# Dealing out the K and Q chains of an attention preparation step by step

## The chip, the cores and the metric

The program runs on the 8 cores of one Trainium2 chip. Each core computes one sample of a batch of 8 with the same program, and no core talks to another. The metric is the device time of the slowest core in microseconds, from one launch to the end. A core has five engines that run side by side, each with its own queue of instructions that it takes in order: TensorE (PE in the profile; PEld is its weight load), VectorE (DVE), ScalarE (ACT), GpSimd (POOL) and SyncE (SP, which here only issues DMAs). They meet through semaphores.

## The reference, cut to what matters

The reference is two layers of a hybrid backbone over 2048 latent tokens and 256 context tokens. The second layer has a multi-head latent attention with 8 heads. Before the attention, queries, keys and values are made from compressed vectors. This preparation is where the change lies:

```python
def mla_q(cq, q_norm, w_uq, qn_gain, angles):
    q = ((rms(cq) * q_norm) @ w_uq).reshape(b, l, N_HEADS, QK_HEAD)      # 768 -> 8 x 96
    q = rms(q) * qn_gain
    return axial_rope(q, *angles)

def mla_kv(ckv, k_rope, kv_norm, w_uk, w_uv, kn_gain, angles):
    ckv_n = rms(ckv) * kv_norm                                           # 256
    k_nope = (ckv_n @ w_uk).reshape(b, l, N_HEADS, QK_NOPE)              # 8 x 64
    v = (ckv_n @ w_uv).reshape(b, l, N_HEADS, V_HEAD)                    # 8 x 64
    k_r = broadcast(k_rope over the heads)                               # 8 x 32
    k = rms(concatenate([k_nope, k_r])) * kn_gain
    return axial_rope(k, *angles) if angles is not None else k, v
```

Keys and values are made for latent and context tokens, queries for latent tokens only, and only the 32 last elements of a head are rotated.

## The kernel before, in words

The program is recorded in stages: modulation vectors, a first mixer, a mixture of experts, then the second layer's mixer with an input projection, an S5 scan, the MLA preparation and attention, and a second mixture of experts. Between stages every engine waits for all others.

Python functions record the instructions. The calls `P.mm`, `P.tr`, `P.act`, `P.dve`, `P.pool` and `P.dma` append an instruction to one engine's list, in the order of the calls, and add a semaphore wait wherever a name in `reads` or `writes` was last touched by another instruction. Nothing reorders the lists later: the order of the Python calls is the order on each engine. `P.mm` writes lines L117 and L119 of the profile, `P.tr` line L125, `P.dma` line L135.

The MLA preparation is the first half of `_cd_mla`. It loops over 18 tiles of 128 tokens: 16 latent tiles with a K and a Q chain, then 2 context tiles with a K chain only. Each tile's compressed vectors (`ckt`, `cqt`) are loaded a tile ahead by GpSimd's queue (`c1_loads`). A chain is:

1. projection on TensorE into PSUM (`psm`): four matmuls for K and V, twelve for Q (six of 512 columns, six of 256);
2. evacuation by ScalarE with the row's scale (L1298 V, L1302 K, L1322 and L1324 Q); VectorE copies the shared rope part into K (L1305);
3. `norm_rope`: squares on GpSimd (L1245), reduction per head on VectorE (L1246), a small scaling (L1247), a square root on ScalarE (L1249), a reciprocal (L1250), two multiplies over 768 elements (L1251, L1253), the rotation (L1256, four small ones L1260, L1264), and a cast of the unrotated part by ScalarE (L1266; L1269 for context tiles);
4. `transpose_store`: eight transposes on TensorE into PSUM (`pst`), a copy by VectorE (L1275) and a store to DRAM by SyncE.

The loop records the whole K chain of a tile, transposes and store included, and then its whole Q chain. `sq`, `hs`, `R1` and `R2` are single buffers that both chains use; `xb` and `xst` are two buffers that take turns; PSUM banks come from rotations `nps` (six) and `npt` (two). `run_zip` stands in the program already: it steps up to `width` generators in turn, one `yield` each.

Of the kernel before, what the change touches and what calls it, by code (L numbers as in the profile page):

```python
# [1184 lines left out]
def _cd_mla(P, G, nc, mst):  # L1185
    AX = mybir.AxisListType.X
    QSCALE = 96.0 ** -0.5
    with ExitStack() as c1:
# [17 lines left out]
        hs = C(_sb(nc, "hs", [128, 4, 8], F32))
        R1 = C(_sb(nc, "R1", [128, 8, 32], F32))
        R2 = C(_sb(nc, "R2", [128, 8, 32], F32))
        xb = [C(_sb(nc, "xb%d" % s, [128, 8, 96], BF16)) for s in range(2)]
        xst = [C(_sb(nc, "xst%d" % s, [128, 8, 128], BF16)) for s in range(2)]  # L1210
# [33 lines left out]
        def norm_rope(src, sk, gain, gk, dst, dk, t, rope):
            P.pool(lambda e: e.tensor_tensor(out=sq[:], in0=src[:], in1=src[:], op=ALU.mult), reads=[sk], writes=["sq"])  # L1245
            P.dve(lambda e: e.tensor_reduce(out=hs[:, 0, :], in_=sq[:], axis=AX, op=ALU.add), reads=["sq"], writes=["hs"])  # L1246
            P.dve(lambda e: e.tensor_scalar(out=hs[:, 1, :], in0=hs[:, 0, :], scalar1=1.0 / 96, scalar2=EPS, op0=ALU.mult,  # L1247
                                            op1=ALU.add), reads=["hs"], writes=["hs"])
            P.act(lambda e: e.activation(out=hs[:, 2, :], in_=hs[:, 1, :], func=AF.Sqrt), reads=["hs"], writes=["hs"])  # L1249
            P.dve(lambda e: e.reciprocal(out=hs[:, 3, :], in_=hs[:, 2, :]), reads=["hs"], writes=["hs"])  # L1250
            P.dve(lambda e: e.tensor_tensor(out=src[:], in0=src[:], in1=hs[:, 3, :].unsqueeze(2).to_broadcast([128, 8, 96]),  # L1251
                                            op=ALU.mult), reads=[sk, "hs"], writes=[sk])
            P.dve(lambda e: e.tensor_tensor(out=src[:], in0=src[:], in1=gain[:, :].unsqueeze(1).to_broadcast([128, 8, 96]),  # L1253
                                            op=ALU.mult), reads=[sk, gk], writes=[sk])
            if rope:
                P.dve(lambda e: e.tensor_tensor(out=R1[:], in0=src[:, :, 64:96],  # L1256
                                                in1=ropC[:, t, :].unsqueeze(1).to_broadcast([128, 8, 32]), op=ALU.mult),
                      reads=[sk, "rop"], writes=["R1"])
                for (o0, i0) in ((0, 72), (8, 64), (16, 88), (24, 80)):
                    P.dve(lambda e, o0=o0, i0=i0: e.tensor_tensor(  # L1260
                        out=R2[:, :, o0:o0 + 8], in0=src[:, :, i0:i0 + 8],
                        in1=ropS[:, t, o0:o0 + 8].unsqueeze(1).to_broadcast([128, 8, 8]), op=ALU.mult),
                        reads=[sk, "rop"], writes=["R2"])
# [24 lines left out]
        c1_loads(0)
        for t in range(NT):
            s = t % 2  # L1290
            rkv = mst[:, t, 4:5]
# [2 lines left out]
            pkk, psk = nps()
            P.mm(psk[:, :], [(ckt[s][:, k, :], wk[:, k, :]) for k in range(2)], reads=[("ckt", s), "wqkv"], writes=[pkk])
            pkv, psv = nps()
            P.mm(psv[:, :], [(ckt[s][:, k, :], wv[:, k, :]) for k in range(2)], reads=[("ckt", s), "wqkv"], writes=[pkv])
            P.act(lambda e, s=s, psv=psv, rkv=rkv: e.activation(  # L1298
                out=vst[s][:, :, 0:64], in_=psv[:, :].rearrange("p (h e) -> p h e", h=8), func=AF.Identity, scale=rkv),
                reads=[pkv], writes=[("vst", s)])  # L1300
            P.dma("sp", G.vs[t], vst[s][:], reads=[("vst", s)], writes=["dram_v"], semkey="vst%d" % s)
            P.act(lambda e, s=s, psk=psk, rkv=rkv: e.activation(  # L1302
                out=kf[s][:, :, 0:64], in_=psk[:, :].rearrange("p (h e) -> p h e", h=8), func=AF.Identity, scale=rkv),
                reads=[pkk], writes=[("kf", s)])
            P.dve(lambda e, s=s, t=t: e.tensor_copy(out=kf[s][:, :, 64:96],  # L1305
                                                    in_=mst[:, t, 8:40].unsqueeze(1).to_broadcast([128, 8, 32])),
                  writes=[("kf", s)])
            u = ui % 2
            ui += 1
            norm_rope(kf[s], ("kf", s), GK, "GK", xb[u], ("xb", u), t, t < NT_L)  # L1310
            transpose_store(xb[u], ("xb", u), xst[u], ("xst", u),
                            G.ks[:, :, t * 128:(t + 1) * 128].rearrange("h d n -> d h n"), "xst%d" % u)
            if t < NT_L:
                rq = mst[:, t, 3:4]
                qfl = qf[s][:].rearrange("p h e -> p (h e)")
                pka, psa = nps()
                P.mm(psa[:, :], [(cqt[s][:, k, :], wq[:, k, 0:512]) for k in range(6)], reads=[("cqt", s), "wqkv"],
                     writes=[pka])
                pkb, psb = nps()
                P.mm(psb[:, 0:256], [(cqt[s][:, k, :], wq[:, k, 512:768]) for k in range(6)],  # L1320
                     reads=[("cqt", s), "wqkv"], writes=[pkb])
                P.act(lambda e, qfl=qfl, psa=psa, rq=rq: e.activation(out=qfl[:, 0:512], in_=psa[:, :], func=AF.Identity,  # L1322
                                                                      scale=rq), reads=[pka], writes=[("qf", s)])
                P.act(lambda e, qfl=qfl, psb=psb, rq=rq: e.activation(out=qfl[:, 512:768], in_=psb[:, 0:256],  # L1324
                                                                      func=AF.Identity, scale=rq),
                      reads=[pkb], writes=[("qf", s)])
                u = ui % 2
                ui += 1
                norm_rope(qf[s], ("qf", s), GQ, "GQ", xb[u], ("xb", u), t, True)
                transpose_store(xb[u], ("xb", u), xst[u], ("xst", u),  # L1330
                                G.qs[:, :, t * 128:(t + 1) * 128].rearrange("h d n -> d h n"), "xst%d" % u)
# [78 lines left out]
```

How the kernel before makes its waits and increments, by code:

```python
    def _wait(self, X, ev):  # L61
        if ev is None:
            return
        kind, k, v = ev
        key = (kind, k)
        if X.waited.get(key, 0) >= v:
            return
        X.waited[key] = v
        sem = self.eng[k].sem if kind == "e" else self.dsem[k][0]
        X.ins.append(lambda e, sem=sem, v=v: e.wait_ge(sem, v))
        X.sim.append(("w", key, v))
# [20 lines left out]
    def op(self, en, fn, reads=(), writes=()):  # L92
        X = self.eng[en]
        self._deps(X, reads, writes)
        X.tick += 1
        sem = X.sem
        X.ins.append(lambda e, fn=fn, sem=sem: fn(e).then_inc(sem, 1))
        X.sim.append(("i", ("e", en), 1))
        self._commit(("e", en, X.tick), reads, writes, en)
# [10 lines left out]
    def mm(self, out, pairs, reads=(), writes=()):  # L110
        X = self.eng["pe"]
        self._deps(X, reads, writes)
        n = len(pairs)
        sem = X.sem
        for i, (l, r) in enumerate(pairs):
            if i == n - 1:
                X.ins.append(lambda e, l=l, r=r, i=i: e.matmul(out, l, r, start=(i == 0), stop=True).then_inc(sem, 1))
            else:
                X.ins.append(lambda e, l=l, r=r, i=i: e.matmul(out, l, r, start=(i == 0), stop=False))
        X.tick += 1
        X.sim.append(("i", ("e", "pe"), 1))
        self._commit(("e", "pe", X.tick), reads, writes, "pe")
```

## Time and profile before

| what | us |
|---|---|
| median of 6 runs (range) | 11719.06 (11355.41 to 12172.02) |
| the profiled execution, its own time | 11356.62 |
| its span on the slowest core | 11355.1 |
| the other cores' spans | 11321.0 to 11354.5 |
| the MLA preparation's 16 latent tiles, first K matmul to the first one behind them | 527.66 |
| TensorE busy over the span | 8082.0 |

The page gives, for the slowest core, how long each engine is busy, the span in 40 slices, and the costliest groups of instructions with the time that the engine stood idle before them and what ended it. A timeline row has the start in us, the duration in us, engine, line of the program, operation, destination and sources (buffer numbers left out), shapes, and in brackets the idle time before it and who ended it.

### The profile page before, as it was taken

To read this page: it belongs to the slowest core of one execution; us is meant where nothing else is said; L and a number is where in the kernel's file an instruction comes from. 1 tells how busy PE (TensorE), PEld (TensorE's weight loads), DVE (VectorE), ACT (ScalarE), POOL (GpSimd) and SP (SyncE) were. 2 spreads that over 40 slices of the span, in tenths; PEclk is the share of its full clock that TensorE was granted. 3 is DMA by queue.
4 is the path that set the end of the run, shared out by engine and by line. 5 is a ranking of instruction groups with operands and counts; after the bars stand their busy time and mean duration, and the time that the engine had idled before them with its cause. 6 is when DMAs were issued, how large, how long until landed. Compare 5 with 4: busy or idle time off the path is not lost. (4 is left out here: it accounts for less than half of the span.)

```text
span 11355.1 us, 123247 instructions; the slowest of 8 cores (11321.0 to 11355.1 us)
## 1 busy us (share of the span) xinstructions
PE 8082.0 (71%) x37576; PEld 3873.0 (34%) x37576; DVE 6038.8 (53%) x9756; ACT 2191.6 (19%) x3933; POOL 839.7 (7%) x785
## 2 busy tenths in 40 slices
PE   7766489999999999761111111236667999999998
PEld 5322344444444444530000000113333444444443
DVE  0443356666666666117777777330034666666666
ACT  1312311111111111122222222116521111111110
POOL 0000000000000000002222222110000000000000
PEclk8887599999999999575555555557668999999999
DMA  3210022222222211210000000111102222222221
GB/s 108 30 25 15 1 45 34 34 34 34 32 32 34 33 30 20 74 39 1 3 1 3 1 3 3 42 24 28 39 16 41 38 35 43 36 40 39 34 41 45
DMA packets 335979, 344.18 MB, mean 30 GB/s; under 512 B 117427, under 2 KB 262067, under 8 KB 335352
## 3 DMA queue, kind: packets, MB, share of 16 engines
q0 software_dynamic: 200240, 226.18, 13.1%
q1 hardware_dynamic: 135112, 110.12, 3.3%
q8 instruction: 335, 5.49, 0.2%
q14 instruction: 292, 2.39, 0.1%
HBM read 529.35 MB, written 28.74 MB: 49 GB/s over the span
## 5 line engine op out<-in xcount | busy, mean ns | idle before, releaser
L119 PE MATMUL psu_u<-tT_u,wu_u 128*128 128x512 bf16 (+1 forms) x8064 | 1835.1, 367 | 56.7 <-DVE he_u L651 50.3
L119 PE MATMUL psg_u<-tT_u,wg_u 128*128 128x512 bf16 (+1 forms) x8064 | 1837.7, 368 | 49.0 <-DMA wg_u<-moe_w_gate 49.0
L119 PE MATMUL psy_u<-wd_u,he_u 128*128 128x512 bf16 x6528 | 1763.1, 379 | 56.2 <-DVE tmpe_u L356 56.2
L651 DVE TENSOR_TENSOR he_u<-sg_u,psu_u 128x512 bf16<-128x512 f32 (+1 forms) x1152 | 753.7, 657 | 1853.4 <-PE psu_u L117 1849.7
L356 DVE SCALAR_TENSOR_TENSOR tmpe_u<-psy_u,gates_u,gtile_u 128x512 f32<-128x512 f32 x2176 | 1624.1, 746 | 58.5 <-PE psy_u L117 58.5
L649 ACT ACTIVATE sg_u<-psg_u 128x512 f32<-128x512 f32 (+1 forms) x1152 | 660.8, 574 | 5103.7 <-PE psg_u L117 2502.5
L359 DVE TENSOR_TENSOR xl_u<-xl_u,tmpe_u 128x512 f32<-128x512 f32 x2176 | 1506.4, 692 | 226.3
L119 PEld LDWEIGHTS psg_u<-tT_u,wg_u 128*128 128x128 bf16 x8064 | 789.7, 98 | 915.3 <-issue 55.4
L119 PEld LDWEIGHTS psu_u<-tT_u,wu_u 128*128 128x128 bf16 x8064 | 786.9, 98 | 922.5 <-issue 68.4
L119 PEld LDWEIGHTS psy_u<-wd_u,he_u 128*128 128x128 bf16 x6528 | 619.9, 98 | 881.1 <-issue 180.2
L117 PE MATMUL psy_u<-wd_u,he_u 128*128 128x512 bf16 x2176 | 824.5, 379 | 0.0
L119 PE MATMUL pss_u<-s5hr_u,lc_u 128*128 128x512 bf16 x128 | 74.9, 585 | 833.9 <-DVE s5hi_u L1145 804.5
L125 PE MATMUL pss_u<-ident_u,bb_u 128*128 128x128 f32 x64 | 29.3, 458 | 828.0 <-DVE bb_u L1034 828.0
L125 PE MATMUL psm_u<-ident_u,xn_u 128*128 128x128 f32 x560 | 225.4, 441 | 403.7 <-DVE xn_u L298 341.1
L117 PE MATMUL psg_u<-tT_u,wg_u 128*128 128x512 bf16 (+1 forms) x1152 | 423.5, 368 | 0.0
L117 PE MATMUL psu_u<-tT_u,wu_u 128*128 128x512 bf16 (+1 forms) x1152 | 423.5, 368 | 0.0
L125 PE MATMUL pst_u<-identb_u,xb_u 128*96 128x128 bf16 x272 | 84.6, 311 | 381.6 <-ACT xb_u L1266 328.2
L135 POOL DMA_DIRECT2D wg_u<-moe_w_gate x64 | 56.6, 885 | 3813.1 <-PE psg_u L117 3562.8
L119 PEld LDWEIGHTS pss_u<-s5hr_u,lc_u 128*128 128x128 bf16 x128 | 13.3, 104 | 921.3 <-issue 921.3
L1374 ACT ACTIVATE pT_u<-psS_u 128x512 bf16<-128x512 f32 x576 | 318.5, 602 | 43.4 <-PE psO_u L816 29.0
L117 PEld LDWEIGHTS psy_u<-wd_u,he_u 128*128 128x128 bf16 x2176 | 212.4, 98 | 257.2
L125 PEld LDWEIGHTS pss_u<-ident_u,bb_u 128*128 128x128 f32 x64 | 11.6, 182 | 836.3 <-issue 834.3
(300 smaller groups left out, 8357.1 us busy)
## 6 DMA issues: line engine op xcount, KB each, us to landing
wg_u<-moe_w_gate POOLq DMA_DIRECT2D x64, 1024.0 KB, 10.5
wu_u<-moe_w_up POOLq DMA_DIRECT2D x64, 1024.0 KB, 14.6
wd_u<-moe_w_down POOLq DMA_DIRECT2D x64, 1024.0 KB, 8.2
adaw_u<-ada_w SPq DMA_DIRECT2D x24, 2048.0 KB, 7.9
xl_u<-x SPq DMA_DIRECT2D x1, 8192.0 KB, 30.6
out<-xl_u SPq DMA_DIRECT2D x1, 8192.0 KB, 24.3
wB_u<-ab_w_in POOLq DMA_DIRECT2D x24, 256.0 KB, 6.0
zs_scr<-zst_u SPq DMA_DIRECT2D x48, 128.0 KB, 1.7
```

The costliest lines, as they stand in the source:

```text
L117: X.ins.append(lambda e, l=l, r=r, i=i: e.matmul(out, l, r, start=(i == 0), stop=True).then_inc(sem, 1))
L119: X.ins.append(lambda e, l=l, r=r, i=i: e.matmul(out, l, r, start=(i == 0), stop=False))
L125: self.op("pe", lambda e: e.transpose(out, in_, ident), reads, writes)
L135: X.ins.append(lambda e: e.dma_start(out=out, in_=in_, **kw).then_inc(sem, 16))
L356: P.dve(lambda e: e.scalar_tensor_tensor(out=tmp[:, 0:n], in0=ps, scalar=gate, in1=gt[:, r, c0:c0 + n], op0=ALU.mult, op1=ALU.mult), reads ...
L359: P.dve(lambda e: e.tensor_tensor(out=G.xl[:, t, c0:c0 + n], in0=G.xl[:, t, c0:c0 + n], in1=tmp[:, 0:n], op=ALU.add), reads=[tk, ("xl", t) ...
L649: P.act(lambda e, cs=cs, n=n: e.activation(out=sg[cs][:, 0:n], in_=psg[cs][:, 0:n], func=AF.Silu), reads=[("psg", cs)], writes=[("sg", cs)])
L651: P.dve(lambda e, cs=cs, n=n, hs=hs, m=m: e.tensor_tensor(out=he[hs][:, m, 0:n], in0=sg[cs][:, 0:n], in1=psu[cs][:, 0:n], op=ALU.mult), re ...
L1374: P.act(lambda e: e.activation(out=pT[ps_][:], in_=psS[ss][:, :], func=AF.Exp), reads=[("psS", ss)], writes=[("pT", ps_)])
```

## The change

Both chains become Python generators, `k_chain` and `q_chain`, which `yield` after nearly every step, and the tile's two generators go through `run_zip(..., 2)`. K is stepped first in each round, but has one step more ahead of `norm_rope`, so Q is one step ahead there. `sq`, `hs`, `R1`, `R2`, `xb` and `xst` become four buffers each (chain and parity of the tile, `w`), and PSUM banks are fixed: K and V take `psm` 0 and 1, Q 2 and 3, and each chain has a `pst` bank of its own. The arithmetic, the shapes and the number of instructions stay.

```diff
-        sq = C(_sb(nc, "sqh", [128, 8, 96], F32))
...
+        sq = [C(_sb(nc, "sqh%d" % s, [128, 8, 96], F32)) for s in range(4)]
...
-        nps = _rot([C(_ps(nc, "psm%d" % s, [128, 512], F32)) for s in range(6)], "psm")
-        npt = _rot([C(_ps(nc, "pst%d" % s, [128, 1024], BF16)) for s in range(2)], "pst")
+        psf = [C(_ps(nc, "psm%d" % s, [128, 512], F32)) for s in range(5)]
+        ptb = [C(_ps(nc, "pst%d" % s, [128, 1024], BF16)) for s in range(2)]
+        nps = _rot([psf[4]], "psm4")
...
+        def norm_rope(src, sk, gain, gk, dst, dk, t, rope, w):
+            sq_, hs_, R1_, R2_ = sq[w], hs[w], R1[w], R2[w]
+            P.pool(lambda e: e.tensor_tensor(out=sq_[:], in0=src[:], in1=src[:], op=ALU.mult), reads=[sk],
+                   writes=[("sq", w)])
+            yield
+            P.dve(lambda e: e.tensor_reduce(out=hs_[:, 0, :], in_=sq_[:], axis=AX, op=ALU.add), reads=[("sq", w)],
+                  writes=[("hs", w)])
+            yield
...
+                P.dve(lambda e: e.tensor_tensor(out=dst[:, :, 64:96], in0=R1_[:], in1=R2_[:], op=ALU.add),
+                      reads=[("R1", w), ("R2", w)], writes=[dk])
                 P.act(lambda e: e.activation(out=dst[:, :, 0:64], in_=src[:, :, 0:64], func=AF.Identity),
                       reads=[sk], writes=[dk])
+                yield
...
+        def transpose_store(srcb, sbk, stt, stk, dram_view, semk, w):
+            pk, pt = ("pst", w), ptb[w]
             for h in range(8):
                 P.tr(pt[0:96, h * 128:(h + 1) * 128], srcb[:, h, :], identb[:], reads=[sbk, "identb"], writes=[pk])
+            yield
             P.dve(lambda e: e.tensor_copy(out=stt[0:96, :, :], in_=pt[0:96, :].rearrange("p (h n) -> p h n", h=8)),
                   reads=[pk], writes=[stk])
+            yield
             P.dma("sp", dram_view, stt[0:96, :, :], reads=[stk], writes=["dram_qk"], semkey=semk)
+            yield
...
         for t in range(NT):
-            s = t % 2
-            rkv = mst[:, t, 4:5]
             if t + 1 < NT:
                 c1_loads(t + 1)
...
+            run_zip([k_chain(t)] + ([q_chain(t)] if t < NT_L else []), 2)
```

On VectorE, one latent tile of the kernel before has K's chain (`kf`) whole, its copy out of PSUM (`xst`) included, and Q's (`qf`) only after it; the rows are K's end and Q's beginning.

```order
L1251 TENSOR_TENSOR kf_u<-kf_u,hs_u 128x768
L1253 TENSOR_TENSOR kf_u<-kf_u,GK_u 128x768
L1256 TENSOR_TENSOR R_u<-kf_u,ropC_u 128x256
L1260 TENSOR_TENSOR R_u<-kf_u,ropS_u 128x8x8 x4
L1264 TENSOR_TENSOR xb_u<-R_u 128x8x32
L1275 COPY xst_u<-pst_u 96x1024
L1246 TENSOR_REDUCE hs_u<-sqh_u 128x8
L1247 TENSOR_SCALAR hs_u<-hs_u 128x8
L1250 RECIPROCAL hs_u<-hs_u 128x8
L1251 TENSOR_TENSOR qf_u<-qf_u,hs_u 128x768
L1253 TENSOR_TENSOR qf_u<-qf_u,GQ_u 128x768
```

In the changed kernel the same engine has, for a tile with scratch 3 for Q and 1 for K:

```order
L1250 TENSOR_REDUCE hs3_u242<-sqh3_u238 128x8
L1250 TENSOR_REDUCE hs1_u240<-sqh1_u236 128x8
L1253 TENSOR_SCALAR hs3_u242<-hs3_u242 128x8
L1253 TENSOR_SCALAR hs1_u240<-hs1_u240 128x8
L1259 RECIPROCAL hs3_u242<-hs3_u242 128x8
L1259 RECIPROCAL hs1_u240<-hs1_u240 128x8
L1261 TENSOR_TENSOR qf1_u232<-qf1_u232,hs3_u242 128x768
L1261 TENSOR_TENSOR kf1_u234<-kf1_u234,hs1_u240 128x768
L1265 TENSOR_TENSOR qf1_u232<-qf1_u232,GQ_u222 128x768
L1265 TENSOR_TENSOR kf1_u234<-kf1_u234,GK_u223 128x768
```

Each instruction of Q is now followed by the same one of K, on its own buffers, and the copies out of PSUM stand behind both chains.

On TensorE, a tile of the kernel before reads as follows (`wk`, `wv`, `wq` are the projections, `pst` the transposes):

```order
L117 MATMUL psm_u<-wk_u,ckt_u 128x512
L119 MATMUL psm_u<-wv_u,ckt_u 128x512
L117 MATMUL psm_u<-wv_u,ckt_u 128x512
L125 MATMUL pst_u<-identb_u,xb_u 96x128 x8
L119 MATMUL psm_u<-wq_u,cqt_u 128x512 x5
L117 MATMUL psm_u<-wq_u,cqt_u 128x512
L119 MATMUL psm_u<-wq_u,cqt_u 128x256 x5
L117 MATMUL psm_u<-wq_u,cqt_u 128x256
L125 MATMUL pst_u<-identb_u,xb_u 96x128 x8
```

and a tile of the changed one:

```order
L117 MATMUL psm_u<-wk_u,ckt_u 128x512
L119 MATMUL psm_u<-wv_u,ckt_u 128x512
L117 MATMUL psm_u<-wv_u,ckt_u 128x512
L119 MATMUL psm_u<-wq_u,cqt_u 128x512 x5
L117 MATMUL psm_u<-wq_u,cqt_u 128x512
L119 MATMUL psm_u<-wq_u,cqt_u 128x256 x5
L117 MATMUL psm_u<-wq_u,cqt_u 128x256
L125 MATMUL pst_u<-identb_u,xb_u 96x128 x16
```

The transposes of K have moved behind the Q projection, next to those of Q, which come first of the sixteen.

## Rows read from the trace of the kernel before

**Rows 1.** Head of the page.
```profile
span 11355.1 us, 123247 instructions; the slowest of 8 cores (11321.0 to 11355.1 us)
```
**Rows 2.** Busy us (instructions) in the 16 latent tiles, granted clock, DMA share, GB/s.
```profile
7149.35:7677.01 527.66, 166.03 (x513) 71.62 (x513) 185.57 (x399) 67.31 (x131) 69.52 (x62) 0.53 0.10 24
```
**Rows 3.** Groups of lines, MLA preparation: busy us, mean ns | idle before, who ended it.
```profile
L125 PE MATMUL pst_u<-identb_u,xb_u 128*96 128x128 bf16 x272 | 84.6, 311 | 381.6 <-ACT xb_u L1266 328.2 <-ACT xb_u L1269 17.9
```
**Rows 4.** Timeline: the second tile's Q projection, then parts of the third tile.
```profile
7198.58 2.32 PE L119 MATMUL psm_u<-wq_u,cqt_u 128*128 128x512 bf16 x5
...
7215.19 0.61 PE L119 MATMUL psm_u<-wk_u,ckt_u 128*128 128x512 bf16 x1
...
7216.44 0.63 PE L117 MATMUL psm_u<-wv_u,ckt_u 128*128 128x512 bf16 x1
...
7218.60 0.29 DVE L1305 COPY kf_u<-mst_u 128x256 f32<-128x256 f32 x1 [2.37 <-ACT kf_u L1302]
...
7231.13 2.32 PE L119 MATMUL psm_u<-wq_u,cqt_u 128*128 128x512 bf16 x5
...
7235.31 0.47 ACT L1324 ACTIVATE qf_u<-psm_u,mst_u 128x256 f32<-128x256 f32 x1 [0.65 <-PE psm_u L117]
7236.06 1.46 POOL L1245 TENSOR_TENSOR sqh_u<-qf_u 128x768 f32<-128x768 f32 x1 [15.49 <-ACT qf_u L1324]
7237.46 0.74 POOL L135 DMA_DIRECT2D ckt_u<-zs_scr  x1
7237.62 0.95 DVE L1246 TENSOR_REDUCE hs_u<-sqh_u 128x8 f32<-128x768 f32 x1 [5.44 <-POOL sqh_u L1245]
...
7238.68 0.37 DVE L1247 TENSOR_SCALAR hs_u<-hs_u 128x8 f32<-128x8 f32 x1
...
7239.45 0.20 DVE L1250 RECIPROCAL hs_u<-hs_u 128x8 f32<-128x8 f32 x1 [0.40 <-ACT hs_u L1249]
7239.75 0.96 DVE L1251 TENSOR_TENSOR qf_u<-qf_u,hs_u 128x768 f32<-128x768 f32 x1
7240.81 0.96 DVE L1253 TENSOR_TENSOR qf_u<-qf_u,GQ_u 128x768 f32<-128x768 f32 x1
7241.88 0.43 DVE L1256 TENSOR_TENSOR R_u<-qf_u,ropC_u 128x256 f32<-128x256 f32 x1
7242.22 1.21 DVE L1260 TENSOR_TENSOR R_u<-qf_u,ropS_u 128x64 f32<-128x64 f32 x4
7243.53 0.42 DVE L1264 TENSOR_TENSOR xb_u<-R_u 128x256 bf16<-128x256 f32 x1
7244.05 0.63 ACT L1266 ACTIVATE xb_u<-qf_u 128x512 bf16<-128x512 f32 x1 [4.71 <-DVE xb_u L1264]
7244.94 3.53 PE L125 MATMUL pst_u<-identb_u,xb_u 128*96 128x128 bf16 x8 [9.78 <-ACT xb_u L1266]
7248.29 0.60 PE L119 MATMUL psm_u<-wk_u,ckt_u 128*128 128x512 bf16 x1
```
**Rows 5.** Timeline of the S5 scan: two independent multiplies; one beside GpSimd.
```profile
5799.59 0.69 DVE L1108 TENSOR_TENSOR s5gr_u<-pss_u,s5tc_u 128x512 f32<-128x512 f32 x1
5800.19 0.68 DVE L1111 TENSOR_TENSOR s5gi_u<-pss_u,s5tc_u 128x512 f32<-128x512 f32 x1
...
5836.29 2.41 POOL L1055 TENSOR_SCALAR s5ts_u<-s5ts_u 128x2304 f32<-128x2304 f32 x1 [2.90 <-DVE s5ts_u L1053]
5836.65 2.59 DVE L1141 TENSOR_TENSOR s5tmp_u<-s5gi_u,s5tc_u 128x512 f32<-128x512 f32 x1
```
**Rows 6.** Windows, granted clock third from the end: transposes, then three rises.
```profile
7195.20:7198.50 3.30, 2.22 (x8) 1.15 (x8) 0.00 (x0) 0.00 (x0) 0.00 (x0) 0.50 0.00 0
7201.20:7201.50 0.30, 0.30 (x4) 0.23 (x3) 0.00 (x0) 0.08 (x1) 0.00 (x0) 0.73 0.96 184
7235.40:7235.70 0.30, 0.00 (x0) 0.00 (x0) 0.00 (x0) 0.30 (x1) 0.00 (x0) 0.84 0.00 0
7631.40:7631.70 0.30, 0.00 (x0) 0.00 (x0) 0.00 (x0) 0.30 (x1) 0.00 (x0) 0.93 0.00 0
```

More of the change, by code:

```diff
@@ L1204, in _cd_mla @@
         kf = [C(_sb(nc, "kf%d" % s, [128, 8, 96], F32)) for s in range(2)]
-        sq = C(_sb(nc, "sqh", [128, 8, 96], F32))
[L1206 to L1210, printed above, removed]
+        sq = [C(_sb(nc, "sqh%d" % s, [128, 8, 96], F32)) for s in range(4)]
+        hs = [C(_sb(nc, "hs%d" % s, [128, 4, 8], F32)) for s in range(4)]
+        R1 = [C(_sb(nc, "R1_%d" % s, [128, 8, 32], F32)) for s in range(4)]
+        R2 = [C(_sb(nc, "R2_%d" % s, [128, 8, 32], F32)) for s in range(4)]
+        xb = [C(_sb(nc, "xb%d" % s, [128, 8, 96], BF16)) for s in range(4)]
+        xst = [C(_sb(nc, "xst%d" % s, [128, 8, 128], BF16)) for s in range(4)]
         vst = [C(_sb(nc, "vst%d" % s, [128, 8, 65], BF16)) for s in range(2)]
-        nps = _rot([C(_ps(nc, "psm%d" % s, [128, 512], F32)) for s in range(6)], "psm")
-        npt = _rot([C(_ps(nc, "pst%d" % s, [128, 1024], BF16)) for s in range(2)], "pst")
+        psf = [C(_ps(nc, "psm%d" % s, [128, 512], F32)) for s in range(5)]
+        ptb = [C(_ps(nc, "pst%d" % s, [128, 1024], BF16)) for s in range(2)]
+        nps = _rot([psf[4]], "psm4")
         P.dma("sp", nT[:, 0:6], G.mla_q_norm[0].rearrange("(k p) -> p k", p=128), writes=["nT"], semkey="nT",
@@ L1242, in _cd_mla @@
             P.pool(lambda e, s=s: e.memset(vst[s][:, :, 64:65], 1.0), writes=[("vst", s)])
[L1244 to L1254, printed above, removed]
@@ new lines, in norm_rope @@
+        def norm_rope(src, sk, gain, gk, dst, dk, t, rope, w):
[6 more added lines that the diff above has]
+            yield
+            P.dve(lambda e: e.tensor_scalar(out=hs_[:, 1, :], in0=hs_[:, 0, :], scalar1=1.0 / 96, scalar2=EPS,
+                                            op0=ALU.mult, op1=ALU.add), reads=[("hs", w)], writes=[("hs", w)])
+            yield
+            P.act(lambda e: e.activation(out=hs_[:, 2, :], in_=hs_[:, 1, :], func=AF.Sqrt), reads=[("hs", w)],
+                  writes=[("hs", w)])
+            yield
+            P.dve(lambda e: e.reciprocal(out=hs_[:, 3, :], in_=hs_[:, 2, :]), reads=[("hs", w)], writes=[("hs", w)])
+            yield
+            P.dve(lambda e: e.tensor_tensor(out=src[:], in0=src[:],
+                                            in1=hs_[:, 3, :].unsqueeze(2).to_broadcast([128, 8, 96]), op=ALU.mult),
+                  reads=[sk, ("hs", w)], writes=[sk])
+            yield
+            P.dve(lambda e: e.tensor_tensor(out=src[:], in0=src[:],
+                                            in1=gain[:, :].unsqueeze(1).to_broadcast([128, 8, 96]), op=ALU.mult),
+                  reads=[sk, gk], writes=[sk])
+            yield
@@ L1255, in norm_rope @@
             if rope:
-                P.dve(lambda e: e.tensor_tensor(out=R1[:], in0=src[:, :, 64:96],
+                P.dve(lambda e: e.tensor_tensor(out=R1_[:], in0=src[:, :, 64:96],
                                                 in1=ropC[:, t, :].unsqueeze(1).to_broadcast([128, 8, 32]), op=ALU.mult),
-                      reads=[sk, "rop"], writes=["R1"])
+                      reads=[sk, "rop"], writes=[("R1", w)])
+                yield
                 for (o0, i0) in ((0, 72), (8, 64), (16, 88), (24, 80)):
@@ L1260, in norm_rope @@
                     P.dve(lambda e, o0=o0, i0=i0: e.tensor_tensor(
-                        out=R2[:, :, o0:o0 + 8], in0=src[:, :, i0:i0 + 8],
+                        out=R2_[:, :, o0:o0 + 8], in0=src[:, :, i0:i0 + 8],
                         in1=ropS[:, t, o0:o0 + 8].unsqueeze(1).to_broadcast([128, 8, 8]), op=ALU.mult),
-                        reads=[sk, "rop"], writes=["R2"])
-                P.dve(lambda e: e.tensor_tensor(out=dst[:, :, 64:96], in0=R1[:], in1=R2[:], op=ALU.add),
-                      reads=["R1", "R2"], writes=[dk])
+                        reads=[sk, "rop"], writes=[("R2", w)])
@@ L1266, in norm_rope @@
+                yield
+                P.dve(lambda e: e.tensor_tensor(out=dst[:, :, 64:96], in0=R1_[:], in1=R2_[:], op=ALU.add),
+                      reads=[("R1", w), ("R2", w)], writes=[dk])
                 P.act(lambda e: e.activation(out=dst[:, :, 0:64], in_=src[:, :, 0:64], func=AF.Identity),
                       reads=[sk], writes=[dk])
+                yield
             else:
                 P.act(lambda e: e.activation(out=dst[:], in_=src[:], func=AF.Identity), reads=[sk], writes=[dk])
-        def transpose_store(srcb, sbk, stt, stk, dram_view, semk):
-            pk, pt = npt()
+                yield
@@ L1273, in transpose_store @@
+        def transpose_store(srcb, sbk, stt, stk, dram_view, semk, w):
+            pk, pt = ("pst", w), ptb[w]
             for h in range(8):
                 P.tr(pt[0:96, h * 128:(h + 1) * 128], srcb[:, h, :], identb[:], reads=[sbk, "identb"], writes=[pk])
+            yield
             P.dve(lambda e: e.tensor_copy(out=stt[0:96, :, :], in_=pt[0:96, :].rearrange("p (h n) -> p h n", h=8)),
                   reads=[pk], writes=[stk])
+            yield
             P.dma("sp", dram_view, stt[0:96, :, :], reads=[stk], writes=["dram_qk"], semkey=semk)
+            yield
@@ new lines, in k_chain @@
+        def k_chain(t):
+            s = t % 2
+            w = 0
+            rkv = mst[:, t, 4:5]
+            pkk, psk = ("psm", 0), psf[0]
+            P.mm(psk[:, :], [(ckt[s][:, k, :], wk[:, k, :]) for k in range(2)], reads=[("ckt", s), "wqkv"], writes=[pkk])
+            pkv, psv = ("psm", 1), psf[1]
+            P.mm(psv[:, :], [(ckt[s][:, k, :], wv[:, k, :]) for k in range(2)], reads=[("ckt", s), "wqkv"], writes=[pkv])
+            yield
+            P.act(lambda e: e.activation(out=vst[s][:, :, 0:64], in_=psv[:, :].rearrange("p (h e) -> p h e", h=8),
+                                         func=AF.Identity, scale=rkv), reads=[pkv], writes=[("vst", s)])
+            P.dma("sp", G.vs[t], vst[s][:], reads=[("vst", s)], writes=["dram_v"], semkey="vst%d" % s)
+            yield
+            P.act(lambda e: e.activation(out=kf[s][:, :, 0:64], in_=psk[:, :].rearrange("p (h e) -> p h e", h=8),
+                                         func=AF.Identity, scale=rkv), reads=[pkk], writes=[("kf", s)])
+            P.dve(lambda e: e.tensor_copy(out=kf[s][:, :, 64:96],
+                                          in_=mst[:, t, 8:40].unsqueeze(1).to_broadcast([128, 8, 32])),
+                  writes=[("kf", s)])
+            yield
+            yield from norm_rope(kf[s], ("kf", s), GK, "GK", xb[2 * w + s], ("xb", 2 * w + s), t, t < NT_L, 2 * w + s)
+            yield from transpose_store(xb[2 * w + s], ("xb", 2 * w + s), xst[2 * w + s], ("xst", 2 * w + s),
+                                       G.ks[:, :, t * 128:(t + 1) * 128].rearrange("h d n -> d h n"),
+                                       "xst%d" % (2 * w + s), w)
@@ new lines, in q_chain @@
+        def q_chain(t):
+            s = t % 2
+            w = 1
+            rq = mst[:, t, 3:4]
+            qfl = qf[s][:].rearrange("p h e -> p (h e)")
+            pka, psa = ("psm", 2), psf[2]
+            P.mm(psa[:, :], [(cqt[s][:, k, :], wq[:, k, 0:512]) for k in range(6)], reads=[("cqt", s), "wqkv"],
+                 writes=[pka])
+            pkb, psb = ("psm", 3), psf[3]
+            P.mm(psb[:, 0:256], [(cqt[s][:, k, :], wq[:, k, 512:768]) for k in range(6)],
+                 reads=[("cqt", s), "wqkv"], writes=[pkb])
+            yield
+            P.act(lambda e: e.activation(out=qfl[:, 0:512], in_=psa[:, :], func=AF.Identity, scale=rq),
+                  reads=[pka], writes=[("qf", s)])
+            P.act(lambda e: e.activation(out=qfl[:, 512:768], in_=psb[:, 0:256], func=AF.Identity, scale=rq),
+                  reads=[pkb], writes=[("qf", s)])
+            yield
+            yield from norm_rope(qf[s], ("qf", s), GQ, "GQ", xb[2 * w + s], ("xb", 2 * w + s), t, True, 2 * w + s)
+            yield from transpose_store(xb[2 * w + s], ("xb", 2 * w + s), xst[2 * w + s], ("xst", 2 * w + s),
+                                       G.qs[:, :, t * 128:(t + 1) * 128].rearrange("h d n -> d h n"),
+                                       "xst%d" % (2 * w + s), w)
@@ L1285, in c1_loads @@
                       writes=[("cqt", s)], semkey="cqt%d" % s)
-        ui = 0
         c1_loads(0)
         for t in range(NT):
-            s = t % 2
-            rkv = mst[:, t, 4:5]
             if t + 1 < NT:
                 c1_loads(t + 1)
[L1294 to L1331, printed above, removed]
```

## The prediction

> **What bounds the kernel now.** I read the head of the page, then busy time by stretch, then the groups of lines of one stretch, then the timeline of one token tile, and last the granted clock in small windows. The reader should see five things.
>
> First, the profiled execution took 11356.62 us around a span of 11355.1 us [rows 1], so 1.5 us lie outside the span. Six timed runs have a median of 11719.06 us, 362 us above it; three of them lie within 9 us of the profiled one. I forecast an execution like the profiled one.
>
> Second, the change touches one stretch alone, the MLA preparation. Its sixteen latent tiles run from 7149.35 to 7677.01 us [rows 2]: 527.66 us, so 32.98 us for each tile, 4.6% of the span. The two context tiles behind them have a K chain only, and keep the order they have.
>
> Third, nothing is busy there. In 527.66 us TensorE works 166 us, VectorE 186, ScalarE 67 and GpSimd 70 [rows 2]. What fills the time is one chain of dependent steps that walks from engine to engine. The group of the transposes says so: TensorE stands 381.6 us before them, waiting for ScalarE's cast [rows 3].
>
> Fourth, why that wait cannot be filled. Every engine takes its instructions in the order written. The transposes of K wait at TensorE's head, and the Q projection stands behind them though its operands are there. In the timeline the first Q matmul starts at 7231.13, the next K matmul at 7248.29 [rows 4]: one chain is 16 to 17 us long and two stand end to end.
>
> Fifth, TensorE runs mostly at its lower level: granted clock 0.53 over the stretch [rows 2], that is 1.2 GHz with short rises to 2.4.
>
> **The change part by part.** It deals out both chains step by step, so that on each engine an instruction of Q is followed by the same one of K, and gives each chain its own scratch. No arithmetic is added. I add up the longest path of one tile, from its first K matmul to the next tile's, with durations of rows 4, at the lower clock:
>
> 1. Projections. The four K and V matmuls take 1.68 us (7215.19 to 7216.44, and 0.43 for the last). Q's twelve follow at once; from the first of them to ScalarE's second Q evacuation is 4.18 (7231.13 to 7235.31). Together 5.86. K's evacuation now stands behind Q's on ScalarE. That costs nothing: K's squares have to wait for Q's on GpSimd anyway.
> 2. Squares. 0.75 to the start of Q's square (7236.06), then two squares of 1.46, and 0.10 to the reduction: 9.63 at the start of K's reduction. Q's reduction lies under K's square.
> 3. Statistics. Q's small scaling stands behind K's reduction, whose issue I put at 0.87 (below); 0.77 to the reciprocal (7238.68 to 7239.45), 0.30 to the first multiply, 0.15 for K's reciprocal in between: 11.72.
> 4. Multiplies. Four of 768 elements. In one chain they start 1.06 apart (7239.75 to 7240.81), each waiting for the last. Between independent ones a shorter step is seen: 0.34 for 256 elements (7241.88 to 7242.22), 0.60 for 512 [rows 5], so by the same 0.26 per 256 elements I estimate 0.87 for 768. Four are 3.48: 15.20.
> 5. Rotation. Two of 256 elements at 0.34; two groups of four small ones, 1.31 each alone (7242.22 to 7243.53) of which some 0.18 is the wait for the last one and is filled now, so 2.26; then 0.52 to ScalarE's cast and 0.89 to the first Q transpose: 19.55.
> 6. Transposes. Both groups of eight are behind one another on TensorE, with the next tile's K matmuls behind both: 3.35 each (7244.94 to 7248.29), 6.70, and the sum is 26.25 us.
>
> So the chains lie beside each other from the squares to the casts; the projections and the sixteen transposes remain on the path, 12.6 us of it. That is why one chain's length is not reached.
>
> Two small terms stand beside this. The first: GpSimd overlaps VectorE now. K's rope copy (0.29, at 7218.60) falls beside Q's square, and Q's reduction beside K's square. In S5 a VectorE multiply that started beside a GpSimd instruction took 2.59 us against 0.69 and ended 0.54 after that instruction's end [rows 5]: it waited for it. If the copy waits so for Q's square, K's square starts 0.5 later; if Q's reduction waits for K's square, everything behind is 0.87 later. There is nothing to gain here, since both instructions run unhindered now. I take 0.5 for the copy, because even a small scaling grew beside a GpSimd DMA issue (0.37 at 7238.68), and nothing for the reduction, because Q's kept its 0.95 beside such an issue (7237.46 and 7237.62).
>
> The Trainium skill, page "SBUF — State Buffer", section "Who interferes with whom", says that GpSimd and VectorE exclude each other for a whole instruction when VectorE reads two SBUF inputs beside a GpSimd read, or copies in a two-port mode, and that a reduction never contends. By that rule the copy can pay and the reduction doesn't, so the sum would be the one below; without the rule's lock it would be 8 us less. The S5 rows bear out its first half; no row here shows a reduction beside a GpSimd square.
>
> The second: the clock rose ten times in the stretch, the first time at 7201.2 and the last at 7631.4 [rows 6], each time 2.6 to 4.3 us after the first Q matmul (7198.58, 7231.13), and it stayed at 0.50 through the transposes ahead of them. Now 5.5 us of projection matmuls follow without a gap. A rise 2.6 to 5.5 us into them halves what is left: 0 to 1.5 us; I take 0.6. Were it up from the first K matmul, it would be 2.8.
>
> Other edits are at nothing: the extra scratch buffers (no wait in rows 4 is for a buffer), fixed PSUM banks instead of a rotation (each is read 20 us before it is written again), q_scr ahead of k_scr on SyncE's queue (nothing reads either before the stretch ends), and GpSimd's loads, which still stand a tile ahead.
>
> Sum: 26.25 + 0.5 - 0.6 = 26.15 us a tile, 6.83 less than 32.98; times sixteen 109 us. 11356.62 - 109 = 11247 us, 1.0% faster, which is inside the 2% that a measurement of this kernel can about tell from no change.
>
> The ends: with 1.06 between all five 768-element steps (+0.95), no fill in the rotation (+0.36), copy and reduction both held (+1.37) and no rise, 28.93 us, 65 us gained: 11292. With the clock up from the first K matmul and no contention, 23.5 us, 152 gained: 11205.
>
> **The rivals.**
> - Clock up for all projections (0.10): 11205 as above. For it: TensorE is now busy 12.6 us without a pause. Against it: through the transposes the clock stayed at 0.50 [rows 6].
> - VectorE fills little and GpSimd holds it (0.12): without the two holds of GpSimd 27.56 us a tile, with both 28.93, which is 11270 to 11292. For it: the 2.59 us row. Against it: in S5 independent multiplies keep a 0.60 step.
> - It does not overlap (0.03): some wait I took for filled holds a whole engine, as the transposes did before: 11357. Against it: the order of VectorE, where Q and K alternate instruction by instruction.
> - Slower (0.03): GpSimd holds up VectorE's two-operand instructions. The place is the two squares and the two DMA issues of each tile, 4.5 us of GpSimd; the price up to 1.9 for each instruction caught [rows 5]. The point is 6.83 / 1.9, so four a tile: 33.75, or five: 35.65 us and 11399. Against it: by the sum above the first multiply starts 2.2 us after K's square ends.
> - Over 2% faster (0.04) needs 18.8 us a tile, below everything worked out here; over 2% slower (0.03) needs 47. These two are for what no row shows.
>
> **How the numbers follow.** The forecast has 0.65, with its own range of 11215 to 11285. The range of 11200 to 11300 takes in the first two rivals and leaves out 0.13 of cases and the odds of a size I got wrong. Faster by over 2% 0.04, slower by over 2% 0.03, so 0.93 within.
>
> **What would show it.** In the profile after, the first K matmuls of successive tiles should stand 25 to 27 us apart, sixteen tiles should take about 418 us, TensorE's transposes should come sixteen in a row, and its idle time before them should be about 14 us a tile once rather than 10 us twice. Multiplies of 768 elements should start 0.87 apart. Granted clock should rise late in most Q projections. I am wrong if the spacing of tiles is above 30 (then look for stretched VectorE rows or a late square), below 23.5 (then the transposes have shrunk too), or if time moves outside this stretch.

## The result, and the profile after

| what | before, us | after, us |
|---|---|---|
| median of the runs | 11685.15 (16 runs) | 11248.23 (8 runs) |
| lowest and highest | 11354.25, 12172.02 | 11233.46, 11756.54 |
| span of the profiled execution | 11355.1 | 11243.5 |
| sixteen latent tiles of the preparation | 527.66 | 418.04 |

The ratio is 0.9865 with a 95% interval of 0.980 to 0.993: faster by 0.7 to 2.0%. In many executions the cores of one die (0 to 3, or 4 to 7) or of both show a lower granted clock and take longer, so the medians are not to be compared, and what follows reads the sixteen tiles, whose time is nearly the same on all cores, and spans of cores at the higher clock. The interval rests on few runs: the mean of the three shortest runs of before is 11357.8, that of the six short ones of after 11244.9, a ratio of 0.990; with the next run of before, 11521.39, among them it is 0.9865.

The head of the page and the windows of the changed kernel, to be held beside [rows 1, 2]: busy us (instructions) of PE, PEld, DVE, ACT and POOL, then granted clock, DMA share and GB/s.

```profile
span 11243.5 us, 123204 instructions; the slowest of 8 cores (11210.8 to 11243.5 us)
```

```profile
7151.02:7569.06 418.04, 157.78 (x513) 72.10 (x513) 185.90 (x399) 64.21 (x131) 69.54 (x62) 0.59 0.12 30
```

The work is the same: VectorE was busy 185.57 us and is 185.90, GpSimd 69.52 and 69.54. Only the stretch is shorter, by 109.62 us. The span fell by 111.6 us, so all but 2 us of it lies here. A tile takes 26.13 us (418.04 / 16). This is the slowest core; on the eight cores of this profile the sixteen tiles take 415.3 to 418.0 us, 416.2 in the median, where before they took 526.8 to 527.9.

The group of the transposes, beside [rows 3]: idle time behind the bar, and who ended it.

```profile
L125 PE MATMUL pst_u<-identb_u,xb_u 128*96 128x128 bf16 x272 | 83.7, 311 | 280.1 <-ACT xb_u L1282 226.9 <-ACT xb_u L1286 17.7
```

TensorE waited 328.2 us for the casts of the latent tiles and now waits 226.9: once a tile, 14.2 us, where it was twice 10.

One tile in the timeline, beside [rows 4]: start, duration, engine, line, operation, and in brackets the idle time before and who ended it.

```profile
7229.31 0.61 PE L119 MATMUL psm_u<-wk_u,ckt_u 128*128 128x512 bf16 x1
...
7234.75 0.47 ACT L1338 ACTIVATE qf_u<-psm_u,mst_u 128x256 f32<-128x256 f32 x1 [0.20 <-PE psm_u L117]
...
7235.44 1.46 POOL L1247 TENSOR_TENSOR sqh_u<-qf_u 128x768 f32<-128x768 f32 x1 [21.44 <-ACT qf_u L1338]
7235.91 1.14 DVE L1315 COPY kf_u<-mst_u 128x256 f32<-128x256 f32 x1 [5.55 <-ACT kf_u L1313]
7237.00 0.95 DVE L1250 TENSOR_REDUCE hs_u<-sqh_u 128x8 f32<-128x768 f32 x1
7237.26 1.46 POOL L1247 TENSOR_TENSOR sqh_u<-kf_u 128x768 f32<-128x768 f32 x1 [0.36 <-DVE kf_u L1315]
...
7238.82 0.95 DVE L1250 TENSOR_REDUCE hs_u<-sqh_u 128x8 f32<-128x768 f32 x1 [0.87 <-POOL sqh_u L1247]
...
7239.69 0.57 DVE L1253 TENSOR_SCALAR hs_u<-hs_u 128x8 f32<-128x8 f32 x2
...
7240.96 0.96 DVE L1261 TENSOR_TENSOR qf_u<-qf_u,hs_u 128x768 f32<-128x768 f32 x1
7241.84 0.95 DVE L1261 TENSOR_TENSOR kf_u<-kf_u,hs_u 128x768 f32<-128x768 f32 x1
7242.71 0.95 DVE L1265 TENSOR_TENSOR qf_u<-qf_u,GQ_u 128x768 f32<-128x768 f32 x1
7243.57 0.95 DVE L1265 TENSOR_TENSOR kf_u<-kf_u,GK_u 128x768 f32<-128x768 f32 x1
7244.44 0.42 DVE L1270 TENSOR_TENSOR R_3_u<-qf_u,ropC_u 128x256 f32<-128x256 f32 x1
...
7247.36 0.42 DVE L1280 TENSOR_TENSOR xb_u<-R_3_u 128x256 bf16<-128x256 f32 x1
...
7248.76 7.06 PE L125 MATMUL pst_u<-identb_u,xb_u 128*96 128x128 bf16 x16 [14.16 <-ACT xb_u L1282]
...
7255.65 0.60 PE L119 MATMUL psm_u<-wk_u,ckt_u 128*128 128x512 bf16 x1
```

Read it down the VectorE rows: Q and K alternate, and four multiplies start 0.87 apart (7240.96, 7241.84, 7242.71, 7243.57). The copy of the rope part lasts 1.14 us, against 0.29 in [rows 4]. It starts inside Q's square and ends 0.15 after the square's end, and K's square starts after that, with GpSimd idle for 0.36. The transposes come sixteen in a row.

Windows around rises of the clock in three tiles, beside [rows 6]; the granted clock, a share of full speed, is third from the end.

```profile
7206.60:7206.90 0.30, 0.30 (x3) 0.13 (x2) 0.00 (x0) 0.10 (x1) 0.00 (x0) 0.83 0.64 137
...
7233.60:7233.90 0.30, 0.30 (x3) 0.24 (x2) 0.00 (x0) 0.04 (x1) 0.00 (x0) 0.50 0.00 0
7233.90:7234.20 0.30, 0.30 (x4) 0.23 (x3) 0.00 (x0) 0.30 (x1) 0.00 (x0) 0.82 0.00 0
7261.20:7261.50 0.30, 0.17 (x1) 0.00 (x0) 0.00 (x0) 0.00 (x0) 0.00 (x0) 0.81 0.00 0
```

The clock rose from 1.2 to 2.4 GHz in each of the sixteen tiles; before, it rose in ten. The first K matmuls of these three stand at 7203.96, 7229.31 and 7255.65, so it came 2.6, 4.6 and 5.6 us behind them, and those tiles took 25.35, 26.34 and 26.68 us. The five tiles in which the rise came 2.6 to 2.9 us behind the first K matmul took 24.98 to 25.70 us, the eleven in which it came 4.3 to 5.6 us behind took 26.14 to 26.68.

### The profile page after: what moved, and what is told of

The parts are those of the page before. It is cut to its first block and busy times, and to the rows that moved or that the text cites. A ratio compares the mean times of both kernels' runs of the same rounds, so it can differ in the third digit from the quotient of the medians.

```text
span 11243.5 us, 123204 instructions; the slowest of 8 cores (11210.8 to 11243.5 us)
## 1 busy us (share of the span) xinstructions
PE 8085.7 (72%) x37576; PEld 3876.7 (34%) x37576; DVE 6039.6 (54%) x9756; ACT 2192.0 (19%) x3933; POOL 839.6 (7%) x785
## 5 line engine op out<-in xcount | busy, mean ns | idle before, releaser
L119 PEld LDWEIGHTS pss_u<-s5hr_u,lc_u 128*128 128x128 bf16 x128 | 13.3, 104 | 921.1 <-issue 921.1
L117 PE MATMUL psS_u<-qh_u,kh_u 96*128 96x512 bf16 x576 | 290.0, 507 | 10.8 <-DMA kh_u<-k_scr 10.2
```

The costliest lines, as they stand in the source:

```text
L117: X.ins.append(lambda e, l=l, r=r, i=i: e.matmul(out, l, r, start=(i == 0), stop=True).then_inc(sem, 1))
L119: X.ins.append(lambda e, l=l, r=r, i=i: e.matmul(out, l, r, start=(i == 0), stop=False))
```

## The experiments

The theory under test: the gain comes from two chains lying beside each other from the squares to the casts; what is left of a tile is the projections, the squares and sixteen transposes, on which nothing lies. The tiles of each run are those of one core, the executions are all that were timed.

| run | sixteen latent tiles, us (core) | executions, us |
|---|---|---|
| in turn again | 526.63 (3) | 11363.16 |
| only Q's projection ahead | 487.59 (5) | 11725.88 |
| rope copy early | 410.17 (1), 409.85 (7) | 11485.08 to 11753.67 (three) |
| one event for eight transposes | 327.95 (4) | 11390.81 |
| next tile begun early | 278.57 (4) | 11098.79, 11427.38 |
| all three together, first timing | 212.42 (0) | 11339.50 to 12076.50 (five) |
| second timing | 211.99 (6) | 11149.28 to 12129.08 (five) |
| third timing | 212.21 (0) | 11142.64 to 11458.20 (four) |
| changed kernel, second timing | 416.46 (6) | 11540.41 to 12253.46 (six) |
| changed kernel, third timing | 416.28 (0) | 11271.10 to 12104.60 (five) |

### In turn again, with the new buffers

```diff
-            run_zip([k_chain(t)] + ([q_chain(t)] if t < NT_L else []), 2)
+            run_zip([k_chain(t)] + ([q_chain(t)] if t < NT_L else []), 1)
```

> The changed kernel with its four-fold scratch and fixed banks, but each tile's K chain recorded whole before its Q chain. Theory (the gain comes from the two chains lying beside each other): the sixteen latent tiles take 527 us again (32.9 to 33.1 a tile), the span about 11355. Rival (private scratch and fixed banks carry part of it): below 510 us.

The window of its sixteen tiles:

```profile
7153.05:7679.68 526.63, 166.00 (x514) 71.70 (x513) 185.81 (x399) 67.56 (x131) 69.53 (x62) 0.54 0.10 24
```

526.63 us, and the slowest core's span 11361.6, the kernel before within 0.1% of the span and 0.2% of the stretch. Private scratch and fixed banks carry nothing by themselves; the gain comes with the order. Whether the order would bring it with the shared scratch was not run.

### Only Q's projection moved ahead

```diff
-            run_zip([k_chain(t)] + ([q_chain(t)] if t < NT_L else []), 2)
+            q = q_chain(t) if t < NT_L else None
+            if q is not None:
+                next(q)
+                next(q)
+            run_zip([k_chain(t)] + ([q] if q is not None else []), 1)
```

> Chains in turn, but Q's projection and its two evacuations are recorded ahead of K's chain, so nothing of Q's projection stands behind K's transposes. Theory (what fills VectorE's and GpSimd's waits makes the gain, not the projection's place): of 32.98 us a tile only the projection leaves the second chain, 3.85 us come back ahead of the first, VectorE's copy out of PSUM comes between: about 31.6 us a tile, 505 us for sixteen. Rival (TensorE's queue was the loss): below 440 us.

The timeline of one tile on core 0: Q's square, then K's end and Q's beginning.

```profile
7657.70 1.46 POOL L1247 TENSOR_TENSOR sqh_u<-qf_u 128x768 f32<-128x768 f32 x1
...
7665.09 3.53 PE L125 MATMUL pst_u<-identb_u,xb_u 128*96 128x128 bf16 x8 [10.84 <-ACT xb_u L1282]
7668.79 0.69 DVE L1294 COPY xst_u<-pst_u 96x1024 bf16<-96x1024 bf16 x1 [4.68 <-PE pst_u L125]
7669.40 0.94 DVE L1250 TENSOR_REDUCE hs_u<-sqh_u 128x8 f32<-128x768 f32 x1
...
7676.50 3.53 PE L125 MATMUL pst_u<-identb_u,xb_u 128*96 128x128 bf16 x8 [7.89 <-ACT xb_u L1282]
7679.85 2.32 PE L119 MATMUL psm_u<-wq_u,cqt_u 128*128 128x512 bf16 x5
```

487.59 us on core 5, the slowest, and 486.9 to 489.5 on all eight; fifteen tiles take 30.7 us each and the last 26.78. The rival falls: with Q's operands evacuated and squared long before (7657.70), Q's reduction still starts at 7669.40, behind VectorE's copy, which waits for K's transposes. The in-order queue that held Q was VectorE's as much as TensorE's; taking the projection out of TensorE's queue brings 40 of the 110 us. My number was 17 us too high: 0.9 us in each of the fifteen tiles, and 4.8 in the last, since the context tile behind it has no Q projection ahead of its first K matmul. A part of the 0.9 may be the clock, which in this tile rises at K's first matmul (0.50 up to 7653.0, 1.00 from 7653.6); that was not taken apart.

### The rope copy early

```diff
+            P.dve(lambda e: e.tensor_copy(out=kf[s][:, :, 64:96],
+                                          in_=mst[:, t, 8:40].unsqueeze(1).to_broadcast([128, 8, 32])),
+                  writes=[("kf", s)])
             pkk, psk = ("psm", 0), psf[0]
...
-            P.dve(lambda e: e.tensor_copy(out=kf[s][:, :, 64:96],
-                                          in_=mst[:, t, 8:40].unsqueeze(1).to_broadcast([128, 8, 32])),
-                  writes=[("kf", s)])
             yield
```

> The copy of the shared rope part into K is recorded before the projections instead of behind K's evacuation, so it no longer falls beside Q's square. Theory (the square holds it, and K's square waits 0.36 us for it): copy 0.29 us instead of 1.14, K's square at once behind Q's, 0.36 us a tile less, sixteen tiles about 412 us instead of 418.0. Rival (the hold is hidden elsewhere): 418.

Its timeline on core 7, whose clock was 0.823 (the last row is the copy for the next tile):

```profile
7228.55 1.46 POOL L1247 TENSOR_TENSOR sqh_u<-qf_u 128x768 f32<-128x768 f32 x1 [20.74 <-ACT qf_u L1338]
7229.98 1.46 POOL L1247 TENSOR_TENSOR sqh_u<-kf_u 128x768 f32<-128x768 f32 x1
7230.11 0.95 DVE L1250 TENSOR_REDUCE hs_u<-sqh_u 128x8 f32<-128x768 f32 x1 [5.76 <-POOL sqh_u L1247]
...
7249.59 0.28 DVE L1304 COPY kf_u<-mst_u 128x256 f32<-128x256 f32 x1
```

The copy is 0.28 us again and K's square follows Q's at once, 1.43 behind its start. Sixteen tiles took 409.85 us on this core, 409.68 on core 4 and 410.17 on core 1, the slowest core of the execution: 8 us less than 418.04, where 6 were expected. The median of eight cores falls by 6.5, from 416.2 to 409.7. So the overlap costs about 0.4 us a tile, near the 0.36 of the profile after; the sum had 0.5. The second reading is the reduction: it lies wholly beside K's square and keeps its 0.95.

### One event for eight transposes

```diff
+        def tr_group(pt, srcb, reads, writes):
...
+            for h in range(7):
+                E_.ins.append(lambda e, h=h: e.transpose(pt[0:96, h * 128:(h + 1) * 128], srcb[:, h, :], identb[:]))
+            sem = E_.sem
+            E_.ins.append(lambda e: e.transpose(pt[0:96, 896:1024], srcb[:, 7, :], identb[:]).then_inc(sem, 1))
...
-            for h in range(8):
-                P.tr(pt[0:96, h * 128:(h + 1) * 128], srcb[:, h, :], identb[:], reads=[sbk, "identb"], writes=[pk])
+            tr_group(pt, srcb, reads=[sbk, "identb"], writes=[pk])
```

> The changed kernel, but the eight transposes of a group signal once at the last instead of each, so none waits for the one before. Theory (they start 0.46 us apart because each waits for its forerunner's event, and all sixteen are on the path): apart by 0.13 to 0.20, 4.2 to 5.3 us a tile less, sixteen tiles 335 to 352 us. Rival (0.31, the length of one, is the floor): 2.4 us a tile less, 380 us. Rival (they are hidden): 418 us.

Its timeline at the transposes, and the window of the sixteen tiles:

```profile
7233.54 0.95 PE L1293 MATMUL pst_u<-identb_u,xb_u 128*96 128x128 bf16 x7 [14.32 <-ACT xb_u L1282]
...
7234.29 0.31 PE L1295 MATMUL pst_u<-identb_u,xb_u 128*96 128x128 bf16 x1
...
7234.40 0.95 PE L1293 MATMUL pst_u<-identb_u,xb_u 128*96 128x128 bf16 x7
...
7235.14 0.31 PE L1295 MATMUL pst_u<-identb_u,xb_u 128*96 128x128 bf16 x1
```

```profile
7153.02:7480.97 327.95, 97.19 (x505) 57.67 (x512) 185.86 (x400) 63.81 (x131) 69.65 (x62) 0.64 0.16 37
```

Seven transposes go from start to start in 0.75 us, 0.11 each, where they were 0.46 apart. Sixteen tiles take 327.95 us, 90 less than 418.04, or 5.6 a tile. Of that, 5.2 lie in the transposes: from the first of the sixteen to the next tile's K projection it is 1.63 us instead of 6.83, in the mean. The other 0.4 lies ahead of them, where the clock now rises earlier in most tiles. So all sixteen transposes were on the path, and three quarters of their time was the wait of each for the event of the one before. This is nearly as much again as the change itself brought. It is read in the stretch alone; the total of 11390.81 came at a clock of 0.81.

### The next tile begun early

```diff
+        act = []
+        nxt = 0
+        while nxt < NT or act:
+            if nxt < NT and (not act or act[-1][1] >= 8):
+                act.append([tile(nxt), 0])
+                nxt += 1
...
```

`tile(nxt)` steps both chains of a tile, one step each a round. In `transpose_store` three empty steps stand ahead of the copy out of PSUM.

> The changed kernel, with the next tile's chains begun when a tile has done 8 of its steps, and the copy out of PSUM recorded three steps later. Theory (what is left of a tile is the path of projections, squares and transposes that nothing lies beside): the tile falls from 26.1 us to the busiest engine plus some waits, TensorE 12.9 us (5.5 projections, 7.4 transposes), VectorE 11.5: 15 to 18 us a tile, 240 to 290 us for sixteen. Rival (GpSimd's overlap with two-operand VectorE instructions takes it back): GpSimd's 4.5 us a tile on top, above 320.

```profile
7154.54:7433.11 278.57, 145.62 (x497) 67.30 (x497) 194.59 (x384) 65.65 (x129) 69.63 (x62) 0.65 0.19 44
```

That row is the window of its sixteen tiles: 278.57 us, in the range expected for the sixteen; after the first two a tile takes 17.2 to 18.7, where 15 to 18 were expected. VectorE is busy 70% of it instead of 44%. The shorter of its two executions, with a clock of 0.83 on all cores, took 11098.79 us, 258 us less than the 11356.62 of before. What had been left of a tile was path, not work.

### All three together

The staggered tiles with one event for eight transposes and the early copy.

> The staggered tiles with one event for eight transposes and the early rope copy. TensorE falls to about 7.3 us a tile, VectorE's 11 bind: 12.5 to 15 us a tile, 200 to 240 us for sixteen, ratio to the kernel before 0.971 to 0.975. Rival (GpSimd holds VectorE): above 270 us, ratio above 0.977.

The window of its sixteen tiles on core 0, the group of the small rotation multiplies of Q, and a GpSimd square with the multiply beside it:

```profile
7133.29:7345.71 212.42, 101.86 (x488) 57.28 (x496) 190.23 (x380) 65.56 (x129) 70.44 (x62) 0.62 0.24 57
```

```profile
L1275 DVE TENSOR_TENSOR R_u<-qf_u,ropS_u 128x64 f32<-128x64 f32 x60 | 40.9, 682 | 4.7
```

```profile
7349.56 1.73 POOL L1247 TENSOR_TENSOR sqh_u<-kf_u 128x768 f32<-128x768 f32 x1 [8.90 <-ACT kf_u L1328]
7349.89 1.68 DVE L1270 TENSOR_TENSOR R_u<-qf_u,ropC_u 128x256 f32<-128x256 f32 x1
```

212.42 us, 13.3 a tile, and VectorE is busy 90% of it: now it is the bound. GpSimd's squares meet two-operand multiplies here. Q's small ones take 682 ns in the mean, but the mean mixes two kinds: the median is 226 ns, the length of one alone, and the longest takes 1521, about a square's length. Over 60 of them that is 27 us more than their length alone. A larger one is held too: the 256 elements at 7349.89 take 1.68 us where they take 0.42 alone. The rival's mechanism is real and its price is in the stretch, but the stretch stays below the 270 us that it was given. The ratio could not be had from this timing: the shortest of its five executions took 11339.50.

> The staggered kernel with one event and the early copy once more. VectorE was 94% busy in its stretch of 212 us, so 315 us less than the kernel before if the rest stays: ratio 0.972, about 11040 us. If the rest gives some back, above 0.977.

The 94% in this expectation is the share in 7170 to 7340 us; over the whole stretch it is 90%.

> The staggered kernel with one event and the early copy, for its total time, which the two timings before did not give undisturbed: the undisturbed die of the second stood at 11004 to 11030 us, so 11030 us, ratio 0.971. If the other die's cores are slower for a reason of this kernel, 11150 again.

In the shortest execution of the second timing the cores of one die had spans of 11004 to 11030 us and those of the other 11076 to 11147; in the shortest of the third it was the other way round.

```profile
core 0: 11024.0 us, clock 0.829
core 1: 11006.0 us, clock 0.830
core 2: 11023.9 us, clock 0.829
core 3: 10996.7 us, clock 0.830
core 4: 11114.1 us, clock 0.819
core 5: 11140.8 us, clock 0.818
...
die 0 (median of its cores): 11015.0 us, clock 0.830
```

These are the spans by core of the third. In nine of the fourteen executions of this kernel one die has a clock of 0.83, and the slowest of its four cores stands at 11022 to 11039 us: 316 to 333 us less than 11355.1, or 2.8 to 2.9%, and 1.8 to 2.0% less than the changed kernel's 11243.5. The longer die changed sides, and the sixteen tiles take 211 to 213 us on all eight cores of both profiles, so its extra time lies outside the changed stretch. Still, the shortest execution took 11142.64, the expectation's other sign, and why both dies never had 0.83 at once is not shown.

### The changed kernel timed again

> The changed kernel unaltered, timed again beside the kernel before. If the change is the 110 us of the preparation and nothing else, the ratio is 0.990. If more goes than the preparation shows, it is at 0.9865 or below. Sixteen tiles 418 us in the profile either way.

> The changed kernel unaltered, once more beside the kernel before, since the last timing had only disturbed executions. Change worth the preparation alone: ratio 0.990 and 418 us for sixteen tiles. More elsewhere: 0.9865 or below.

The six executions of the first of these timings took 11540.41 us and more, so they say nothing on the ratio; the stretch was 416.46 us. In the profile of the second, one die had a clock of 0.82: its spans are 11205.0 to 11240.5 us, as in the first profile (11210.8 to 11243.5), and the stretch is 416.28 on its first core. 11240.5 against 11355.1 is 0.990, the preparation alone. Its shortest execution took 11271.10, but beside it none of before was under 11609.50. The totals do not settle between 0.990 and 0.9865; these spans and the stretch speak for 0.990.

## Why the prediction was right or wrong

**The time and the mechanism: right.** 11247 was forecast and the median is 11248.23; a tile was to take 26.15 us and takes 26.13; sixteen tiles 418 and 418.04. That it agrees so closely is luck, since the eight cores differ by 2.7 us over the sixteen tiles and the terms miss by up to 0.4. Going through an ordinary tile, 7229.31 to 7255.65, which took 26.34 where the sum without the clock term is 26.75:

- Projections: 5.86 to the second evacuation, 5.44 measured, because the clock rose in them.
- Squares: 9.63 and 0.5 for the held copy, 9.51 measured at K's reduction (7238.82). The copy was held as forecast; the cost was 0.36 in the profile after and about 0.4 by the early-copy run.
- Statistics: 2.09 from K's reduction to the first multiply; 2.14.
- Multiplies: 3.48 for four; 3.48. The step of 0.87 was worked out from 0.34 and 0.60 and came out.
- Rotation to the first transpose: 4.35; 4.32.
- Transposes: 6.70; 6.89.

**The clock term: right in size.** 0.6 was taken from bounds of 0 to 1.5. If a tile with a late rise (26.68) stands for the lower level, the mean of 26.13 says 0.55. The mechanism was too cautious: a rise came in every tile, not in most. No run holds the clock apart from the order.

**Costs at nothing: right as far as tested.** The in-turn run shows that buffers and banks neither give nor take. The order of the stores and the loads were not tested apart.

**The step that failed** is the last one of the sum: "1.0% faster, which is inside the 2% that a measurement of this kernel can about tell from no change". The gain was sized rightly and the noise was not. 2% is 227 us; the shortest runs lie far closer together than that, before 11354.25 to 11363.78 (three), after 11233.46 to 11251.34 (six), 10 and 18 us wide with 103 us between the two groups, and the measured interval, 0.980 to 0.993, does not hold 1. A gain of 109 us should have been forecast as one that shows. The 0.93 was for a time within 2%, and the measured ratio lies there; what it passed over is that a gain smaller than 2% can still be told from none. I had the first of these ranges in hand and did not use it. I also misread it a little: of the six timed runs two, not three, lie within 9 us of the profiled one (11355.41 and 11363.78).

**The rivals.** "Clock up for all projections" fell, since the clock rose 2.6 us behind the first matmul at the earliest. "VectorE fills little" fell with the step of 0.87. "It does not overlap" and "slower" fell with the stretch. What they named did show elsewhere: GpSimd held two-operand multiplies once the tiles were staggered, the small ones for up to 1521 ns against 226 alone.

## What to carry to other kernels

Where a stretch has no busy engine, write down the path of one round with the start-to-start steps of the trace; dealing out a second chain gains only the steps that it lies beside, and what both chains do in one go (here projections and transposes, 12.3 of 26 us) stays on the path twice. Then look at what is left for waits that guard nothing: eight transposes into eight separate slices of one bank need one event, and that edit was worth 90 us beside the change's 110. Before a small gain is called unmeasurable, look how far the shortest runs lie apart.

## What the runs showed of the hardware that I had not expected

- Transposes of 128 x 96 that need not wait for one another start 0.11 us apart at a granted clock of 0.50 (one-event run, 7233.5 to 7235.5); a wait for the own engine's last event makes it 0.46.
- A copy of 256 elements on VectorE that meets a GpSimd square takes 1.14 us instead of 0.28 and ends 0.15 after the square, while a reduction that meets one keeps 0.95. This agrees with the Trainium skill, page "SBUF — State Buffer", section "Who interferes with whom", in both halves, the second of which no row before the change had shown. That this copy runs in a two-port mode, which that rule asks for, no row shows.
- Two-operand multiplies on VectorE that meet a GpSimd square are held for up to about its length, small or not: 64 elements, 0.23 us alone, took up to 1.52, and 256 elements 1.68 instead of 0.42.
